# Output projection and feed-forward of a hybrid decoder step over 544 token columns instead of 560

## What is computed

```
x = concat([meta_tokens, x_prompt])            # 528 rows; the samples apart, 32 rows
...                                            # input projection, attention heads, mLSTM heads
def finish_layer(x, a_heads, m_out, ...):      # D_MODEL 2048, D_FF 8192
    a = rms_norm(a_heads, attn_out_norm) * (1 - lam_init)
    x = x + concat([a, m_out]) @ w_out         # m_out = rms_norm(h, g) * sigmoid(og)
    hf = rms_norm(x, norm_ffn) @ w_up
    return x + square(relu(hf)) @ w_down
y_prompt = xp[:, N_META:]                      # the 16 meta rows are dropped here
```

## Time and profile before

| | |
|---|---|
| median of 3 runs | 4069.4 us (4063.27 to 4069.78) |
| the profiled execution, time | 4076.02 us |
| its span, first to last instruction | 4074.3 us |
| mean granted TensorE clock | 0.953 |
| TensorE busy | 3692.7 us (91%) |
| VectorE, ScalarE, GpSimd busy | 1819.7, 1289.7, 716.5 us |
| data moved by DMA | 575.85 MB, mean 141 GB/s |
| heads normed and output projection | 2176 to 2442 us of the span |
| feed-forward | 2445 to 4053 us |
| last stage | 4055 to 4074 us |

### The profile page before, as it was taken

How to read it: one execution, slowest core, us unless ns; L and a number is a source line. 1 busy time by engine, 2 the same in 40 slices (tenths; PEclk the granted TensorE clock), 3 DMA queues, 4 the chain that set the end, 5 groups by cost and what they waited for, 6 DMA issues and landing times. The chain is left out here.

```text
span 4074.3 us, 66509 instructions
## 1 busy us (share of the span) xinstructions
PE 3692.7 (91%) x26474; PEld 3422.8 (84%) x26474; DVE 1819.7 (45%) x2859; ACT 1289.7 (32%) x1872; POOL 716.5 (18%) x436
## 2 busy tenths in 40 slices
PE   7999996666797999999985999999999999999998
PEld 7999994455686777777762999999999999999998
DVE  4222223774545666676665334333333333333333
ACT  3111111332105777777762113111221111122211
POOL 0000000000004777777782000000000000000000
PEclk9999997777868999999997999999999999999999
DMA  7433422325537888888883422222222222222221
GB/s 202 112 105 106 113 78 97 102 59 183 110 125 241 303 304 300 302 296 301 299 268 102 138 72 84 90 87 83 83 83 83 84 91 86 83 83 83 83 83 65
DMA packets 461513, 575.85 MB, mean 141 GB/s; under 512 B 38486, under 2 KB 333444, under 8 KB 460732
## 3 DMA queue, kind: packets, MB, share of 16 engines
q1 hardware_dynamic: 461276, 572.54, 44.7%
HBM read 521.68 MB, written 50.80 MB: 141 GB/s over the span
## 5 line engine op out<-in xcount | busy, mean ns | idle before, releaser
L1631 POOL TENSOR_TENSOR dc_vl<-dc_vpages,dc_vh 128x1024 fp32r<-128x1024 f32 x256 | 608.8, 2382 | 87.5 <-ACT dc_vh L1964 81.4
L67 PE MATMUL f_acc<-hidden_hi,ffn_lo 128*128 128x280 f32 x2048 | 603.7, 295 | 11.2 <-DVE hidden_lo L2368 11.2
L69 PE MATMUL f_acc<-hidden_hi,ffn_hi 128*128 128x280 f32 x2048 | 599.3, 293 | 0.0
L67 PE MATMUL f_acc<-xf_hi,ffn_lo 128*128 128x280 f32 x2048 | 598.3, 292 | 0.9 <-DVE xf_lo L2398 0.2
L68 PE MATMUL f_acc<-hidden_lo,ffn_hi 128*128 128x280 f32 x2048 | 598.3, 292 | 0.0
L69 PE MATMUL f_acc<-xf_hi,ffn_hi 128*128 128x280 f32 x2048 | 596.2, 291 | 0.0
L68 PE MATMUL f_acc<-xf_lo,ffn_hi 128*128 128x280 f32 x2048 | 595.2, 291 | 0.0
L67 PE MATMUL z_acc<-xn_hi,win_lo 128*128 128x280 f32 x1536 | 448.0, 292 | 1.1 <-DVE win_lo L300 1.1
L69 PE MATMUL z_acc<-xn_hi,win_hi 128*128 128x280 f32 x1536 | 449.0, 292 | 0.0
L68 PE MATMUL z_acc<-xn_lo,win_hi 128*128 128x280 f32 x1536 | 447.6, 291 | 0.0
L2337 ACT ACTIVATE ffn_hi<-ffn_raw 128x2048 fp32r<-128x2048 f32 x127 | 242.4, 1908 | 637.2 <-PE f_acc L69 637.2
(11 more groups left out here) (360 smaller groups left out, 6381.0 us busy)
## 6 DMA issues: line engine op xcount, KB each, us to landing
dc_kpages<-in_cache_k SPq DMA_DIRECT2D x256, 512.0 KB, 5.0
dc_vpages<-in_cache_v SPq DMA_DIRECT2D x256, 512.0 KB, 4.7
ffn_raw<-in_w_up SPq DMA_DIRECT2D x64, 1024.0 KB, 6.3
ffn_raw<-in_w_down SPq DMA_DIRECT2D x64, 1024.0 KB, 5.0
win_raw<-in_w_in SPq DMA_DIRECT2D x48, 1024.0 KB, 6.1
ffn_raw<-in_w_out SPq DMA_DIRECT2D x16, 1024.0 KB, 6.3
z_scratch<-z_out SPq DMA_DIRECT2D x48, 280.0 KB, 2.4
sm_c<-in_state_C SPq DMA_DIRECT2D x32, 256.0 KB, 4.6
```

Source lines behind the costliest of these rows:

```text
L67: nc.tensor.matmul(out, wlo, xhi, start=first, stop=False)
L69: return nc.tensor.matmul(out, whi, xhi, start=False, stop=last)
L1631: G.tensor_tensor(vl[:, m % VBUF, :], vring[:, m % RING, :], vh[:, m % VBUF, :].bitcast(F32), ALU.subtract).then_inc(vlo, 1)
```

## The change

The two stages work on 544 columns, 16 to 559 of `mix`, as a slice. `Dims` gets `to = t - 16 = 544` and `ohalf = 272`. The buffers of the two stages (split operands, squares, gate, root, hidden features, `sumsq`) are made 544 wide. The loads of the gate and of the residual take the columns from 16 on. Every other access to a half of the columns is 272 wide instead of 280. The columns 0 to 15 of `mix` keep what the heads left in them.

```
+        self.to = self.t - N_META
+        self.ohalf = self.to // 2
...
-    T, E, NH, N, GROUP = d.t, d.md // P, d.ha + d.hm, d.kc, Flow.RAW
+    T, E, NH, N, GROUP = d.to, d.md // P, d.ha + d.hm, d.kc, Flow.RAW
...
-                sp.dma_start(og[:, h, :, :], ogv[cog // E + h]).then_inc(og_in[h], 16)
+                sp.dma_start(og[:, h, :, :], ogv[cog // E + h][:, :, N_META:d.t]).then_inc(og_in[h], 16)
...
-            sp.dma_start(xt[:, :, :], x_dram.rearrange("(k p) t -> p k t", p=P)).then_inc(residual_in, 16)
+            sp.dma_start(xt[:, :, :], x_dram.rearrange("(k p) t -> p k t", p=P)[:, :, N_META:d.t]).then_inc(residual_in, 16)
...
-            nc.vector.tensor_tensor(x, x, acc[j % 2][:, :, 0:d.half], ALU.add).then_inc(added, 1)
+            nc.vector.tensor_tensor(x, x, acc[j % 2][:, :, 0:d.ohalf], ALU.add).then_inc(added, 1)
...
-                cs = slice(h * d.half, (h + 1) * d.half)
+                cs = slice(h * d.ohalf, (h + 1) * d.ohalf)
...
-                    mm = exact_passes(nc, acc[j][:, h, 0:d.half], whi[:, k, :], wlo[:, k, :], mhi[:, k, cs],
+                    mm = exact_passes(nc, acc[j][:, h, 0:d.ohalf], whi[:, k, :], wlo[:, k, :], mhi[:, k, cs],
...
-        hid = sb("hidden", [P, 2, d.t])
-        hhi, hlo = (sb(f"hidden_{x}", [P, G, d.t], F32R) for x in ("hi", "lo"))
-        root, rstd, over = sb("ffn_root", [P, d.t]), sb("ffn_rstd", [P, d.t]), sb("ffn_over_width", [P, P])
+        hid = sb("hidden", [P, 2, d.to])
+        hhi, hlo = (sb(f"hidden_{x}", [P, G, d.to], F32R) for x in ("hi", "lo"))
+        root, rstd, over = sb("ffn_root", [P, d.to]), sb("ffn_rstd", [P, d.to]), sb("ffn_over_width", [P, P])
...
-                            mm = exact_passes(nc, acc[j % 2][:, h, 0:d.half], whi[:, k, :], wlo[:, k, :],
+                            mm = exact_passes(nc, acc[j % 2][:, h, 0:d.ohalf], whi[:, k, :], wlo[:, k, :],
...
-                    mhi = four.enter_context(nc.sbuf_tensor("mix_hi", [P, d.kc, d.t], F32R))
-                    mlo = four.enter_context(nc.sbuf_tensor("mix_lo", [P, d.kc, d.t], F32R))
+                    mhi = four.enter_context(nc.sbuf_tensor("mix_hi", [P, d.kc, d.to], F32R))
+                    mlo = four.enter_context(nc.sbuf_tensor("mix_lo", [P, d.kc, d.to], F32R))
...
-                        finish_and_project(nc, d, a, sems, c, z_dram, mix, mhi, mlo, xt_dram, ffn, sumsq)
+                        finish_and_project(nc, d, a, sems, c, z_dram, mix[:, :, N_META:d.t], mhi, mlo, xt_dram, ffn, sumsq)
...
-                xhi = three.enter_context(nc.sbuf_tensor("xf_hi", [P, d.kc, d.t], F32R))
-                xlo = three.enter_context(nc.sbuf_tensor("xf_lo", [P, d.kc, d.t], F32R))
+                xhi = three.enter_context(nc.sbuf_tensor("xf_hi", [P, d.kc, d.to], F32R))
+                xlo = three.enter_context(nc.sbuf_tensor("xf_lo", [P, d.kc, d.to], F32R))
                 with stage(nc) as sems:
-                    mlp(nc, d, a, sems, xhi, xlo, mix, ffn, sumsq)
+                    mlp(nc, d, a, sems, xhi, xlo, mix[:, :, N_META:d.t], ffn, sumsq)
```

More of the change, by code:

```diff
@@ L2100, in _ @@
                 sp.wait_ge(gated, (h - 1) * E)
-                sp.dma_start(og[:, h % 2, :, :], ogv[cog // E + h]).then_inc(og_in[h % 2], 16)
+                sp.dma_start(og[:, h % 2, :, :], ogv[cog // E + h][:, :, N_META:d.t]).then_inc(og_in[h % 2], 16)
             sp.wait_ge(lo_made, d.kc)
-            sp.dma_start(xt[:, :, :], x_dram.rearrange("(k p) t -> p k t", p=P)).then_inc(residual_in, 16)
+            sp.dma_start(xt[:, :, :], x_dram.rearrange("(k p) t -> p k t", p=P)[:, :, N_META:d.t]).then_inc(residual_in, 16)
             with sp.Fori(0, N // GROUP - 1) as g:
@@ L2215, in _ @@
             dve.wait_ge(summed, d.kc)
-            V.tensor_scalar(two(root[:, :]), mean[0:NH, :, 0:d.half], EPS, None, ALU.add).then_inc(rooting, 1)
+            V.tensor_scalar(two(root[:, :]), mean[0:NH, :, 0:d.ohalf], EPS, None, ALU.add).then_inc(rooting, 1)
             dve.wait_ge(rooted, 1)
@@ L2229, in _ @@
                 dve.wait_ge(spread_ready, h + 1)
-                V.scalar_tensor_tensor(two(mix[:, n, :]), two(mix[:, n, :]), gain, spread[h % 2][:, :, 0:d.half],
+                V.scalar_tensor_tensor(two(mix[:, n, :]), two(mix[:, n, :]), gain, spread[h % 2][:, :, 0:d.ohalf],
                                        ALU.mult, ALU.mult).then_inc(scaled, 1)
@@ L2266, in _ @@
                 for b in range(2):
-                    mm = nc.tensor.matmul(mean[0:NH, b, 0:d.half], gather[:, int(n >= d.ha), NH - 1 - h:2 * NH - 1 - h],
-                                          sq[i % 2][:, b * d.half:(b + 1) * d.half], start=(i == 0),
+                    mm = nc.tensor.matmul(mean[0:NH, b, 0:d.ohalf], gather[:, int(n >= d.ha), NH - 1 - h:2 * NH - 1 - h],
+                                          sq[i % 2][:, b * d.ohalf:(b + 1) * d.ohalf], start=(i == 0),
                                           stop=(i == d.kc - 1))
@@ L2276, in _ @@
                 for b in range(2):
-                    mm = nc.tensor.matmul(spread[h % 2][:, b, 0:d.half], scatter[:, h, :],
-                                          inv[:, b * d.half:(b + 1) * d.half], start=True, stop=True)
+                    mm = nc.tensor.matmul(spread[h % 2][:, b, 0:d.ohalf], scatter[:, h, :],
+                                          inv[:, b * d.ohalf:(b + 1) * d.ohalf], start=True, stop=True)
                 mm.then_inc(spread_ready, 1)
@@ L2364, in hidden @@
                 dve.wait_ge(flow.used, g * 32 + 4 * (j + 1))
-                nc.vector.scalar_tensor_tensor(halves(hid[:, j % 2, :]), acc[j % 2][:, :, 0:d.half], 0.0,
+                nc.vector.scalar_tensor_tensor(halves(hid[:, j % 2, :]), acc[j % 2][:, :, 0:d.ohalf], 0.0,
                                                halves(rstd[:, :]), ALU.max, ALU.mult).then_inc(relued, 1)
@@ L2376, in add @@
                     nc.vector.tensor_tensor(halves(xt[:, oc, :]), halves(xt[:, oc, :]),
-                                            acc[2 + i % 2][:, :, 0:d.half], ALU.add).then_inc(added, 1)
+                                            acc[2 + i % 2][:, :, 0:d.ohalf], ALU.add).then_inc(added, 1)
             def split(g, i):
@@ L2401, in _ @@
                     dve.wait_ge(meaned, 1)
-                    nc.vector.tensor_scalar(halves(root[:, :]), mean[:, :, 0:d.half], EPS, None,
+                    nc.vector.tensor_scalar(halves(root[:, :]), mean[:, :, 0:d.ohalf], EPS, None,
                                             ALU.add).then_inc(shifted, 1)
@@ L2442, in run @@
                             for h in range(2):
-                                cs = slice(h * d.half, (h + 1) * d.half)
+                                cs = slice(h * d.ohalf, (h + 1) * d.ohalf)
                                 for k in ks:
-                                    mm = exact_passes(nc, acc[2 + i % 2][:, h, 0:d.half], whi[:, k, ws], wlo[:, k, ws],
+                                    mm = exact_passes(nc, acc[2 + i % 2][:, h, 0:d.ohalf], whi[:, k, ws], wlo[:, k, ws],
                                                       hhi[:, k, cs], hlo[:, k, cs], k == 0, k == G - 1)
@@ L2449, in _ @@
             for h in range(2):
-                mm = nc.tensor.matmul(mean[:, h, 0:d.half], over[:, :], sumsq[:, h * d.half:(h + 1) * d.half],
+                mm = nc.tensor.matmul(mean[:, h, 0:d.ohalf], over[:, :], sumsq[:, h * d.ohalf:(h + 1) * d.ohalf],
                                       start=True, stop=True)
@@ L2555, in build @@
                 decode_attention(nc, d, a, sems, c, zn_dram, tokens(v_sample), mix)
-            sumsq = three.enter_context(nc.sbuf_tensor("ffn_sumsq", [P, d.t], F32))
+            sumsq = three.enter_context(nc.sbuf_tensor("ffn_sumsq", [P, d.to], F32))
             with stage(nc) as ffn_sems:
```

## The result

The changed kernel took 4035.45 us (median of 4 runs, 4029.12 to 4041.49) beside 4067.65 for the kernel before (4 runs), a ratio of 0.9914 (0.9901 to 0.9927): 32 us faster, where 52.5 had been forecast. The direction was right, and the forecast gain 15 to 20 us too large.

The account below looks back on a forecast made before the run. TensorE's matmul starts were taken to bound the last two stages. Savings of 51.1 - 0.1 + 1.1 + 0 + 0.4 = 52.5 us, against a median of 4069.4, gave 4016.9 us, range 4010 to 4025 (76%), widened 4005 to 4031.

Parts of the forecast that it names:

- term 2: TensorE's wait in each feed-forward group for the last quarter of hidden features: grows 7 ns x 16, 0.1 us, counted as nothing.
- term 5: Residual load of 4,480 KB, awaited by the first addition: 3.8 us of slack, so taken as 0.
- Term 4: Head norms, where TensorE waits for VectorE: shorter operations and smaller gate loads save 1.1 us together.
- Term 6: Start of the feed-forward, where TensorE follows xf_lo block by block: 0.3 us saved, plus 0.1 for the residual sums' tail.
- the prediction's own signs of being wrong: Distance above 127 or below 124.5 ns, a TensorE wait in the projection's second tile, or untouched earlier stages taking another time.
- Term 1: 13,824 matmuls in feed-forward and output projection, each 8 columns narrower: 3.7 ns apiece, 51.1 us saved (46.1 to 55.3).
- Term 3: Weight splits keep their size while TensorE's tiles shrink; over 7 us to spare, so cost zero.
- The flat slope: Rival: width hardly sets the matmul distance, so the matmul term is 15.9 us and the time 4052; 7%.
- the steps of 16 columns: Rival: matmul distance falls in steps of 16 columns, so 272 saves 83 to 99 us, 3985 to 3969; 7%.
- The slower case: Rival: new operand places in a row double the 12.2 ns over the clock, 122 us slower, 4190; 3%.
- The give-back by a wait: Rival: a wait, likeliest the residual load at a lower rate, costs 11 us plus a 2 us slow restart: 4030; 7%.

Follow-up runs that it names:

- the two pairs of profiles: Changed kernel and kernel before, both unedited, each profiled twice; head norms to end took 1898.2 and 1896.6 us before, 1855.8 and 1859.7 after.
- the later medians: The changed kernel run again unedited against the kernel before: 4029.87 us beside 4067.37, ratio 0.9902.
- the one spacing tried: Changed kernel with rows of the split operands again 560 elements apart, 544 used; group period 97.77 us instead of 97.86, no median given.
- the kernel with the uneven cut: Changed kernel with its 544 columns cut into 256 and 288 instead of 272 and 272: 4014.41 us beside 4067.33 for the kernel before, ratio 0.9868.

## Why the prediction was wrong

**What held.** The bound (TensorE's starts in the last two stages) was right, and so was the direction. The wait for the hidden features stayed at 11.2 us in 16 times, as term 2 said. Additions of 544 elements take 719 ns, foreseen 720. The residual load took no time from TensorE, as term 5 said. Term 4 came to about what it was put at: up to the first matmul of the projection the head norms took 64.0 us in the result's profile and 65.3 in the second one, 65.7 and 66.2 before, about 1.3 less, foreseen 1.1; over all eight profiles with 544 columns, 64.0 to 65.8, it is 0.9. Term 6, put at 0.4, is hardly there: from the last matmul of the projection to the first of the feed-forward 6.7 us in both kernels, and the first group gained no more than its matmuls. The 4076.0 us of the profiled execution against a median of 4069.4 was mostly the drift of the early stages: the head norms began 7.3 us later than in the second profile of that kernel. The same drift set off one of the prediction's own signs of being wrong, that the stages ahead of the change take another time; it says nothing against the mechanism.

**Term 1 failed, in the choice of the row.** The prediction took 3.7 ns for 8 columns, the middle between 3.33 and 4.0, the second of which the 256-column stream gave, and read 3.33, the clock alone, as its lower bound. The mean of all distances in a group outside the waits went from 128.8 to 125.9: 2.9 ns, below that bound. Two things are in this. The extra of 12 ns does not scale with the width; the run at 240 columns shows it (12.1 ns). That alone takes 3.7 back to 3.33. And the row that seemed nearest, 256, is the one width with less extra, so that it lay under the line and made the slope look steeper. The remaining 0.4 ns is the irregular part of the extra: in the down tiles it stayed the same (129.4 to 126.1, 3.3 ns), in the up tiles, which the projection shares, it rose by 0.9 (128.1 to 125.6, 2.5 ns). By experiment that part moves by up to half a ns with the spacing of rows; what makes it rise at 272 columns is not shown. Between the widths of the table it differs by a ns or more, so no bound on 8 columns was safe to half a ns. The term measured: 12,288 x 2.93 = 36.0 us in the feed-forward and 1,536 x 2.5 = 3.8 in the projection, **39.8 us instead of 51.1**.

**Term 3 failed, by a wait it did not look for.** It asked who waits for the weight split, found 7 us to spare, and costed the step at zero. It did not ask what is queued behind the split on VectorE. That was an addition which TensorE needs at its third block, 0.05 us after it ended in the kernel before. Work of fixed size ahead of it meant that time taken from TensorE there turned into waiting. Moving the addition shows 3.7 us in all, of which the change added 2.0 by the starts.

**The sum.** 39.8 - 2.0 + 1.3 is 39.1 us, with the 39.6 of the two pairs of profiles beside it, and 37.5 by the later medians. So 11.3 of the missing 13.4 us are term 1, and 2.0 are term 3. The first medians showed 32 us; in the one of those executions that was profiled the early stages ran 5.2 us late, and for the others it is likely but not recorded. That part of the miss, some 6 us, is chance. With the second median, 4029.87 us, the forecast of 4010 to 4025 is still missed.

**The rivals.** The flat slope (7%) and the steps of 16 columns (7%) are both off: 240 to 304 columns lie within about 1 ns of one line, except 256, which lies 1.5 under it. The slower case needed a doubled extra from the new places of the rows; the one spacing tried moved the distance by half a ns at most. (Its 127.3 ns for the up tiles, from counts in a window, is 128.1 by the starts, so the spread between up and down tiles was 1.3 ns and not 1.6.) The give-back by a wait came true in kind, but at another place than the residual load and at a sixth of the price (2.0 us, not 13). The range was too narrow at its upper end, since its lower bound on the saving, 46.1, was taken as certain.

## What to carry to other kernels

A narrower matmul saves its columns at the clock, not its share of the measured distance: the part over the clock stays. To get the slope, measure in the same loop, at widths far enough apart that a scatter of a ns does not matter; a row from another stage may sit on an exception. When TensorE gets shorter and a fixed piece of work stays on VectorE, look not only at who waits for this piece, but at what stands behind it. And where columns have to be cut in two anyway, try 256 for one part.

## What the runs showed of the hardware

At the full clock these pairs of weight load and matmul with split fp32r operands start 11.3 to 13.3 ns further apart than columns over 2.4 GHz, at every one of the widths tried from 240 to 304 but one, while at the 1.2 GHz level the extra is gone: 280 columns start 233 ns apart. The distance is not one number. At 272 columns it moves up and down between 120 and 134 ns, in a pattern that comes back with small shifts from tile to tile; its mean in the up tiles was 125.6 ns in each of three profiles. At 256 columns it is nearly even, and takes one of several values: 117.8 ns, or 113.3 for stretches from one wait to another in the same run, and 116.7 in the kernel with the uneven cut.

What sets the value, and why 256 is better than 240, 264 or 288, stays open. Within the run at 256 the place of operands and results is the same at both values, so it does not choose between them. The spacing of rows and the place in PSUM were varied at 272 columns only. The size of the weight load was not varied by any run, but the trace of the kernel before has a case: in the score stream of decode attention every other load has 64 columns instead of 128 and takes 0.13 to 0.14 us instead of 0.19, and the matmuls start 116 to 118 ns apart behind either, 116.9 on average, as 256 columns do in the feed-forward. So at this width the size of the load does not set the distance. With 256 at 113.3 ns throughout, the best cut would give another 1.7 ns on the mean, an estimate of 23 us over 13,824 matmuls, but nothing here shows how to hold it there.
